# First stage of a hybrid block: parameter loads moved from ScalarE's queue to SyncE's, turned input copied by two engines, v's first tile column-tiled

## The reference

```python
z = h @ w_in                                  # 1040 x 1024 times 1024 x 2048
u, q, k, v = z[:, :512], z[:, 512:1024], z[:, 1024:1536], z[:, 1536:]
# S5: 32 groups of 16 channels, 64 complex states each
dt = exp(log_dt); mag = exp(lr * dt); ar = mag * cos(li * dt); ai = mag * sin(li * dt)
bbr = fr * br - fi * bi;  bbi = fr * bi + fi * br
h_t = a * h_{t-1} + bb @ u_t                  # a scan over all tokens
y = gelu(Re(c @ h) + d * u);  y = y * sigmoid(y @ w_glu + b_glu)
```

## Time and profile before

| | |
|---|---|
| median of three runs | 2460.54 us |
| span of the profiled execution, first to last instruction | 2463.3 us |
| its mean granted TensorE clock | 0.945 |
| first stage, u to the last tile of v | about 38 to 350 us |
| TensorE busy, whole program | 2234.1 us (91%) |

### The profile page before, as it was taken

The page is one execution under the profiler, slowest core; times in us unless marked ns, Lnnn a source line. Parts: engine busy times, 40 slices in busy tenths (PEclk is TensorE's granted clock), DMA queues, the critical chain, the costliest instruction groups (busy, mean ns, idle before and its releaser), DMA issues. The chain is left out here.

```text
span 2463.3 us, 33586 instructions
## 1 busy us (share of the span) xinstructions
PE 2234.1 (91%) x13475; PEld 1269.7 (52%) x13475; DVE 776.3 (32%) x1637; ACT 475.8 (19%) x884; POOL 308.1 (13%) x263
## 2 busy tenths in 40 slices
PE   5999978889968999999976999999986999999994
PEld 4687535565545455455533555555544555545541
DVE  5652026554352111111116344444233111111116
ACT  2222114341110000000003344442110000001001
POOL 5343000001101111101003000000100101111102
PEclk9999988789978999999988999999987999999997
DMA  4100010002229999989979211102118999998987
GB/s 152 36 4 32 17 71 1 1 1 57 72 104 390 419 419 420 419 335 406 412 298 310 93 39 38 38 19 54 52 51 350 413 419 420 420 389 353 417 369 293
DMA packets 148201, 529.82 MB, mean 215 GB/s; under 512 B 43875, under 2 KB 66947, under 8 KB 131665
## 3 DMA queue, kind: packets, MB, share of 16 engines
q1 hardware_dynamic: 119232, 490.78, 50.4%
q0 software_dynamic: 13312, 33.84, 3.6%
q10 hardware_dynamic: 15504, 3.08, 0.6%
HBM read 499.99 MB, written 39.98 MB: 219 GB/s over the span
## 5 line engine op out<-in xcount | busy, mean ns | idle before, releaser
L1787 PE MATMUL l_main_pgu<-l_w_ring,l_ex_xT 128*64 128x256 f32 (+1 forms) x4992 | 472.8, 384 | 12.7 <-DMA l_w_ring<-in_l_moe_w_gate 9.5
L1787 PEld LDWEIGHTS l_main_pgu<-l_w_ring,l_ex_xT 128*64 128x64 f32 (+1 forms) x4992 | 285.2, 128 | 189.6 <-issue 40.5
L1833 PE MATMUL l_main_py<-l_w_ring,l_ex_hT 128*64 128x512 f32 (+1 forms) x1248 | 231.9, 595 | 1.9 <-DVE l_ex_hT L1904 1.9
L1784 PE MATMUL l_main_pgu<-l_w_ring,l_ex_xT 128*128 128x512 f32 x384 | 170.1, 596 | 4.8 <-DMA l_w_ring<-in_l_moe_w_gate 4.8
L2245 PE MATMUL lru_pr<-h2T,lru_wz 128*128 128x352 f32 (+1 forms) x480 | 144.3, 461 | 11.6 <-ACTq L2300 11.6
L1900 DVE TENSOR_TENSOR l_ex_hid<-l_ex_sil,l_main_pgu 128x256 f32<-128x256 f32 (+1 forms) x76 | 35.2, 463 | 376.9 <-PE l_main_pgu L1787 279.7
L1904 DVE COPY l_ex_hT<-l_main_ph 128x256 f32<-128x256 f32 (+1 forms) x76 | 35.4, 466 | 366.4 <-PE l_main_ph L1808 366.4
L2263 PE MATMUL lru_pg<-h2T,lru_wz 128*128 128x512 f32 x320 | 148.7, 592 | 0.0
L1833 PEld LDWEIGHTS l_main_py<-l_w_ring,l_ex_hT 128*64 128x64 f32 (+1 forms) x1248 | 69.1, 127 | 132.1 <-issue 124.8
L2245 PEld LDWEIGHTS lru_pr<-h2T,lru_wz 128*128 128x128 f32 x480 | 92.6, 193 | 64.4 <-ACTq L2300 12.0
L1876 ACT ACTIVATE l_ex_sil<-l_main_pgu 128x256 f32<-128x256 f32 (+1 forms) x76 | 31.7, 417 | 468.9 <-PE l_main_pgu L1787 373.2
(11 more groups left out here) (450 smaller groups left out, 2785.2 us busy)
## 6 DMA issues: line engine op xcount, KB each, us to landing
l_w_ring<-in_l_moe_w_gate SPq DMA_DIRECT2D x64, 2048.0 KB, 24.4
l_w_ring<-in_l_moe_w_up SPq DMA_DIRECT2D x64, 2048.0 KB, 30.5
l_w_ring<-in_l_moe_w_down SPq DMA_DIRECT2D x64, 2048.0 KB, 32.5
l_y<-expert_rows SPq DMA_DIRECT2D x32, 512.0 KB, 8.3
h_rows<-H SPq DMA_DIRECT2D x24, 512.0 KB, 5.2
lru_wz<-in_l_w_in SPq DMA_DIRECT2D x20, 512.0 KB, 5.0
H<-h_rows SPq DMA_DIRECT2D x16, 512.0 KB, 10.1
w_in<-in_l_w_in SPq DMA_DIRECT2D x3, 2048.0 KB, 8.1
```

The costliest lines, as they stand in the source:

```text
L1784: last = pe.matmul(out[:], x[:, k, :], w[0][:, k, :], start=k == 0, stop=k == KD - 1)
L1787: last = pe.matmul(out[HALF * h + o:HALF * h + o + m, 0:256], x[:, k, it.at + o:it.at + o + m], w[n][:, k, 256 * h:256 * h + 256], start=k ...
L1833: last = pe.matmul(py[b][HALF * h + o:HALF * h + o + m, :], hT[:, c % 2, HALF * (c // 2) + o:HALF * (c // 2) + o + m], ws[n][:, c, 512 * h ...
```

## The change

1. The loads of w_in's first block, B, C and b_glu move from ACT's queue to SP's, behind the input rows and ahead of w_in's second block. ACT keeps the four small loads of lambda, dt and d.
2. Of each turned tile ACT copies the first half and DVE the second. `hT_copied` becomes `hT_low` and `hT_high`, and PE waits for both. DVE's copies of tiles 0, 1 and 2 stand among its steps for lambda's angle, those of tiles 3 to 8 ahead of L465's step.
3. C is turned (`turn_c`) and copied (`copy_c`) behind the second pair of u instead of ahead of the first.
4. Tile 0 of v is made as four column tiles of 32 PSUM partitions with 128 moving columns each, and copied in four parts.

```diff
+            sp.dma_start(ring[0][:], w_in[:, :, 0:512]).then_inc(w_loaded[0], 16)
+            with nc.allow_non_contiguous_dma(reason="small parameters"):
+                for t, n in ((b_re, "l0_s5_b_re"), (b_im, "l0_s5_b_im")):
+                    sp.dma_start(t[:], A[n].rearrange("(s two) p h -> (two p) s h", two=2)).then_inc(b_loaded, 16)
+                for c, n in enumerate(("l0_s5_c_re", "l0_s5_c_im")):
+                    for two in range(2):
+                        sp.dma_start(c_rows[c][:, :, two, :], A[n].rearrange("(t j) h p -> (j h) t p", j=8)).then_inc(c_loaded, 16)
+                sp.dma_start(b_glu[:], A["l0_s5_b_glu"].rearrange("(t p) -> p t", p=P)).then_inc(bias_loaded, 16)
             sp.dma_start(ring[1][:], w_in[:, :, 512:1024]).then_inc(w_loaded[1], 16)
...
                 if i >= 2:
-                    pe.wait_ge(hT_copied, 2 * (i - 1))
+                    pe.wait_ge(hT_low, i - 1)
+                    pe.wait_ge(hT_high, i - 1)
...
                 last.then_inc(a_ready, 1)
+                if s == C_BEHIND:
+                    turn_c()
...
                 for k in range(KD):
-                    last = pe.matmul(pa[n % 2][0:m, :], tokens[i % 2][:, k, 0:m], ring[1][:, k, :], start=k == 0, stop=k == KD - 1)
+                    if m <= 32:
+                        for g in range(4):
+                            last = pe.matmul(pa[n % 2][32 * g:32 * g + m, 0:P], tokens[i % 2][:, k, 0:m], ring[1][:, k, P * g:P * g + P], start=k == 0, stop=k == KD - 1)
+                    else:
+                        last = pe.matmul(pa[n % 2][0:m, :], tokens[i % 2][:, k, 0:m], ring[1][:, k, :], start=k == 0, stop=k == KD - 1)
...
             def turn(i):
-                t0, m = TILES[i]
                 act.wait_ge(x_turned, i + 1)
-                for h in range(2):
-                    act.copy(hT[:, 4 * h:4 * h + 4, :, t0 // LEAP:(t0 + m) // LEAP],
-                             pb[2 * (i % 2) + h].rearrange("p (k t) -> p k t", k=4)[:, :, 0:m].rearrange("p k (c j) -> p k j c", j=LEAP)).then_inc(hT_copied, 1)
+                act.copy(*hT_half(i, 0)).then_inc(hT_low, 1)
...
+                if m <= 32:
+                    for g in range(4):
+                        part = act.copy(v_rows[0:m, i, P * g:P * g + P], pa[n % 2][32 * g:32 * g + m, 0:P])
+                    part.then_inc(a_copied, 1)
...
+            def turn(i):
+                dve.wait_ge(x_turned, i + 1)
+                dve.tensor_copy(*hT_half(i, 1)).then_inc(hT_high, 1)
```

More of the change, by code:

```diff
@@ L152, in s5_and_projections @@
     (cleared, small_loaded, b_loaded, c_loaded, bias_loaded, lam_rows_ready, lam_turned, lam_ready, dt_ready, x_ready, mag_ready,
-     angle_ready, sin_ready, f_ready, x_turned, hT_copied, c_turned, ca_cleared, m_cleared, w_cleared, c_ready, ca_ready) = map(sem, (
+     angle_ready, sin_ready, f_ready, x_turned, hT_low, hT_high, c_turned, ca_cleared, m_cleared, w_cleared, c_ready, ca_ready) = map(sem, (
         "cleared", "small_loaded", "b_loaded", "c_loaded", "bias_loaded", "lam_rows_ready", "lam_turned", "lam_ready", "dt_ready",
-        "x_ready", "mag_ready", "angle_ready", "sin_ready", "f_ready", "x_turned", "hT_copied", "c_turned", "ca_cleared",
+        "x_ready", "mag_ready", "angle_ready", "sin_ready", "f_ready", "x_turned", "hT_low", "hT_high", "c_turned", "ca_cleared",
         "m_cleared", "w_cleared", "c_ready", "ca_ready"))
@@ L168, in s5_and_projections @@
     K_NEEDS = (3, 5, 7, 8)
+    C_BEHIND = 1
     def schedule():
@@ L183, in schedule, with hT_half @@
         return events
+    def hT_half(i, h):
+        t0, m = TILES[i]
+        return (hT[:, 4 * h:4 * h + 4, :, t0 // LEAP:(t0 + m) // LEAP],
+                pb[2 * (i % 2) + h].rearrange("p (k t) -> p k t", k=4)[:, :, 0:m].rearrange("p k (c j) -> p k j c", j=LEAP))
     rows_of = lambda i: meta_rows[0:N_META, :] if i == 0 else x_rows[:, i - 1, :]
@@ L217, in _, with turn_c @@
                 last.then_inc(x_turned, 1)
[L218 to L224, removed]
+            def turn_c():
+                pe.wait_ge(c_loaded, 64)
+                for c in range(2):
+                    for t in range(4):
+                        last = pe.transpose(py[c][:, P * t:P * t + P], c_rows[c][:, t, :, :].rearrange("p a b -> p (a b)"), K.ident[:])
+                last.then_inc(c_turned, 1)
+            pe.wait_ge(hT_low, NT)
+            pe.wait_ge(hT_high, NT)
             pe.wait_ge(w_loaded[0], 16)
@@ L365, in _, with copy_c @@
                 turn(i)
[L366 to L372, removed]
+            def copy_c():
+                act.wait_ge(c_turned, 1)
+                act.wait_ge(ca_cleared, 1)
+                for c in range(2):
+                    for two in range(2):
+                        rows = slice(64 * two, 64 * two + 64)
+                        src = py[c][rows, :].rearrange("p (s two h) -> p s two h", two=2, h=16)[:, :, two, :]
+                        act.mul(CA[rows, :, 0, c, 16 * two:16 * two + 16], src, (1.0, -1.0)[c]).then_inc(c_ready, 1)
             for s in range(S5_PAIRS):
@@ L375, in _ @@
                 act.copy(u[:, s, :], pa[s % 2][:, 0:STEPS]).then_inc(a_copied, 1)
+                if s == C_BEHIND:
+                    copy_c()
             for q in range(4):
@@ L412, in v @@
                 act.wait_ge(a_ready, n + 1)
-                act.copy(v_rows[0:m, i, :], pa[n % 2][0:m, :]).then_inc(a_copied, 1)
+                if m <= 32:
+                    for g in range(4):
+                        part = act.copy(v_rows[0:m, i, P * g:P * g + P], pa[n % 2][32 * g:32 * g + m, 0:P])
+                    part.then_inc(a_copied, 1)
+                else:
+                    act.copy(v_rows[0:m, i, :], pa[n % 2][0:m, :]).then_inc(a_copied, 1)
             def glu(j):
@@ L441, in _ @@
             dve.wait_ge(lam_ready, 1)
+            turn(0)
             lim = lam[:, 32:48]
@@ L446, in _ @@
             do(tt(S("ph"), lim, S("dt"), ALU.mult))
+            turn(1)
             do(tsc(S("n"), S("ph"), 1.0 / TWO_PI, ROUND_MAGIC, ALU.mult, ALU.add))
@@ L456, in _ @@
             tsc(S("rc"), S("rc"), TWO_PI / 4, None, ALU.add).then_inc(angle_ready, 1)
+            turn(2)
             do(tt(S("den"), S("lr"), S("lr"), ALU.mult), wait=False)
@@ L462, in _ @@
             tt(dd[:], K.ident[:, 0:32].unsqueeze(1).to_broadcast([P, S5_PAIRS, 32]), bc(lam[:, 96:112], 32), ALU.mult).then_inc(dd_ready, 1)
+            for i in range(3, NT):
+                turn(i)
             dve.wait_ge(mag_ready, 2)
```

## The result

The changed kernel took 2437.69 us (median of four runs, 2431.89 to 2443.95), the kernel before 2460.85 beside it (2460.26 to 2462.5): a ratio of 0.9911, 95% interval 0.9891 to 0.9930. Forecast were 2441.2, with 2437 to 2449 as range. The profiled execution is the longest of the four (2443.95, span 2442.2), so the stage is compared inside the traces and the total by the medians. The medians differ by 23.2 us, the end of the first stage by 19.1 in the traces; the other 4.1 lie within the spread of whole runs, as the repetition further down shows.

A forecast was written before the change was run, and what follows sets the result against it. TensorE sets the first stage's end once u begins, held to 38.33 us by ScalarE's load issues. Terms -15.2 + 1.0 - 5.15 = -19.35 us take the median 2460.54 to 2441.2, range 2437 to 2449.

The forecast's parts named there:

- u starts: TensorE, first stage: u begins at 23.1 us rather than 38.33, with bounds of 21.7 and 26.1.
- u, with C inside: TensorE: u's 16 pairs take 56.25 us, plus 1.0 for turning C behind the second pair.
- VectorE's tables end / `bu` comes: VectorE's tables end at 86.9 and `bu` arrives at 88.4, leaving 1.5 us.
- tile 0 of v: TensorE at v: four column tiles run beside each other, 1.84 us instead of 6.99, saving 5.15.
- last copy of the stage, shift: End of the first stage: comes earlier by -15.2 + 1.0 - 5.15 = -19.35 us.
- The largest term: Ahead of u: moving loads off ScalarE and sharing copies brings u's start forward by 15.2 us.
- The wait behind tile 4: TensorE, having turned tiles 3 and 4, waits with tile 5 for VectorE's copy of tile 3, until 18.2.
- The price of a half: Copying half a turned tile takes 0.69 us on VectorE; ScalarE's half is 0.53 us.
- rival 1: TensorE stays slow while turning: u starts at 25.9 and its first 5.4 us run at half rate; 2446.7 us, 10%.
- 2: Column tiles of v don't overlap, so tile 0 gains nothing: 2446.4 us, chance 7%.
- Rival 4: u itself runs at 1.2 GHz, taking up to 56.25 us more: 2497 us, slower; chance 3%.
- Rival 3: Behind the first stage, attention's clock shifts and gives time back, at worst half the gain: 2451 us, 5%.

The follow-up runs named there:

- the repetition further down: The changed kernel once more, unedited, in six runs: 2440.86 us (2436.45 to 2444.06), ratio 0.9929.
- a2: The changed kernel with the loads back on ScalarE's queue: 2450.28 us.
- a1: The kernel before with only the loads moved to SyncE's queue: 2454.44 us.
- a4: The changed kernel with C turned ahead of u again: 2445.9 us.
- b3: Changed kernel with reordered VectorE and ScalarE lists, 20 identity transposes, tiles 0 to 2 ahead of lambda, w_in's block halved, C behind u's fourth pair: 2442.2 us.
- a3: The changed kernel with ScalarE copying both halves of every tile again: 2436.03 us.
- b4: Kernel b3 with GpSimd's clearing of `w_state` moved behind the wait for the factors f: 2435.68 us, ratio 0.9914.
- b2: The changed kernel with tile copies between VectorE's angle and den steps and ScalarE's sine table earlier: 2440.2 us, ratio 0.9930.

## Why the prediction was right, point by point

| step | forecast | measured |
|---|---|---|
| u starts | 23.1 | 22.79 |
| u, with C inside | 56.25 + 1.0 | 57.40 |
| VectorE's tables end / `bu` comes | 86.9 / 88.4 | 86.42 / 88.26 |
| tile 0 of v | 1.84 | 1.87 |
| last copy of the stage, shift | -19.35 | -19.16 |

- **Loads.** The largest term came from ScalarE's issues in front of its first computation; a2 gives the 14 us back by undoing that alone. ScalarE's first activation came at 10.48 (forecast before 11).
- **What ends last ahead of u.** A copy and not a landing, as forecast, with `w_in` only 1.5 us ahead (21.27). The wait behind tile 4 was put down to VectorE's copy of tile 3, and that holds: it ran from 17.25 to 17.93, and the transposes of tile 5 start at 18.08. The row's bracket names ScalarE, whose two copies at 16.85 ran until 17.96, but the second of them is of tile 4, which tile 5 does not wait for. The price of a half was right: 0.69 us on VectorE, 0.59 on ScalarE.
- **Parts together.** The forecast summed them as if each counted alone. They don't: part 1 alone moves the stage's end by 7.7 us (350.8 - 343.1), parts 2 to 4 alone by 5.0, all by 19.1. Part 3 looked like a cost of 1.0 in the sum, yet without it C's landing would have taken 5.2 us at u. The sum came out since each term was worked out with all parts in place.
- **The whole time.** The shift of the stage is what the working earned (-19.35 against -19.16); that the whole time fits as well is in part luck. The two medians of the changed kernel lie 3.5 and 0.3 us below the forecast, and 23.2 and 16.1 below the kernel before beside them. The prediction took 4.9 us for what a measurement can tell and 2.5 for the difference between runs; the kernel before, unchanged, spread over 12.6 us. With this spread a median could have left the range of 12 us though nothing in the working was wrong.
- **Rivals.** The half rate ended within the first 24 transposes (then 8 in 1.06 and 32 in 3.88), so rival 1 fell; 2 fell with tile 0's 1.87; 4 fell with 128 records of u in 7.22 us. Why those first transposes were slow stays open: the granted clock reads 1.00 over them (9 to 16 us). Rival 4's mechanism exists, though: in a1 and a4, behind idle gaps of 3.46 and 4.79 us, u's first microseconds did run at the lower level, for 1 to 2 us of loss. Rival 3's place was right (attention's clock moved) and its sign is not settled: the rest of the program gives or takes some 5 us without any change.
- **Left out.** GpSimd's clearing of `w_state` was not priced. In the changed kernel it runs from 17.40 to 20.92, beside VectorE's copies out of PSUM, which are not held. With its start tied to the fifth tile, it could have met the angle's steps, as in b3, and cost u some microseconds; that it did not was not in the working, and is luck.

## What to carry to other kernels

Ask of each DMA issue what stands behind it in its engine's list: single issues of 128 KB in rows of 64 bytes held their engine for up to 9.93 us here, while megabytes issued earlier were still landing (why they were held was not tried), so such issues belong on a queue with nothing urgent behind. When the earliest wait is removed, look for the transfer that lands last next, and move its consumer behind work that can already run. And when a copy or a small step moves to another engine, look at what the neighbour clears or writes in that stretch.

## What the runs showed of the hardware

- A small VectorE step with one SBUF input (TENSOR_SCALAR) stood still while GpSimd cleared a tile: 3.56 us in b3 instead of 0.17. In a3 the same kind of step was held in the same way (and in a1, for 2.85 us too):

```profile
17.44 2.85 DVE L499 TENSOR_SCALAR s_nr<-s_apow 128x16 f32<-128x16 f32 x1
```

```profile
16.75 3.52 POOL L625 MEMSET s_w_state<- 128x4096 f32 x1 [8.23 <-PE s_pb L231]
```

  Both end within 0.03 us of each other (20.29 and 20.27). A TENSOR_TENSOR with two SBUF inputs was not held (0.69 us beside the clearing in b4, 0.63 alone), nor was a RECIPROCAL with one (0.24 us, in b2). The Trainium skill, "SBUF — State Buffer", section "Who interferes with whom", says this of the port pair that VectorE and GpSimd share: `tensor_scalar` can run in a mode that needs it whole; whoever issues first then has the pair for its whole instruction, and the other is blocked; a step with two SBUF inputs contends only with a GpSimd instruction that reads. The rows of a3 agree: the clearing had begun 0.69 us ahead of the step. In b3 the two start within 0.03 us of each other, so the rows don't tell which issued first.
- Twenty transposes of the identity ahead of the rows brought the full rate for the first tiles in one profile (b4) and not in the other (b3). The granted clock reads 1.00 in both, so it does not tell the two apart. Of idle gaps in front of TensorE's work, those of 0.7 to 1.6 us left the rate as it was (after, a3, b4); those of 3.46 and 4.79 us (a1, a4), and one of 2.47 with 1.56 shortly ahead of it (b3), were followed by half rate with a granted clock of 0.50. What decides between them was not tried.
- This program, unchanged, spread over more than 12 us between runs (before: 2452.66 to 2465.22). In the four profiles shown, attention is longer where its granted clock reads lower (220 and 221 us at 0.76 and 0.77, 213 and 216 at 0.82 and 0.79). Why the clock differs stays open.
